# A hybrid decoder step on one core: a second stretch with turned banks, wide tiles counted singly, and an eviction one scan later

## The chip, the core and the metric

One core of a Trainium2 chip runs the whole kernel. The metric is the time of one execution on the device, in microseconds (us). The names of the engines are those of the profile: PE is TensorE (matmuls), PEld its weight loads, DVE is VectorE, ACT ScalarE, POOL GpSimd, SP the engine that issues most transfers.

## What is computed

One layer of a decoder whose mixing width is split in two: windowed attention with query and key norm for one half, a complex diagonal state-space model for the other; then an output projection and a squared-ReLU MLP. All of it in float32, for 256 prompt positions and 8 x 4 sample positions (288 columns in all). Cut to what the change touches:

```python
def hybrid_layer(x, cache_k, cache_v, h0_re, h0_im, p):
    z = rmsnorm(x, p['attn_norm_g']) @ p['w_in']
    q, k, v, u = split_projection(z)
    q = rmsnorm(q, p['q_norm_g'])
    k = rmsnorm(k, p['k_norm_g'])
    ...
    y_ssm, h_re, h_im = ssm_mixer(u, h0_re, h0_im, A_bar, B_bar, ...)
    g = jax.nn.gelu(y_ssm)
    ...

def ssm_mixer(u, h0_re, h0_im, A_bar, B_bar, C_re, C_im, D_skip):
    bu = jnp.einsum('ntgh,gph->ntgp', uf.astype(jnp.complex64), B_bar)
    bu = bu.at[:, 0].add(A_bar * h0)
    _, h = lax.associative_scan(ssm_combine, (a, bu), axis=1)
    y = jnp.real(jnp.einsum('ntgp,ghp->ntgh', h, C)) + D_skip * uf
    ...
```

## The kernel before

**Order of the work.** The kernel is written engine by engine, each with its own instruction list in fixed order, and semaphores between them. Weights arrive in steps of 512 KB in four slots. Up to about 200 us TensorE multiplies in full float32: `gemm_full` (four wide tiles per row of weights) and `gemm_half` (two wide tiles per row of weights, so that a unit's first two PSUM banks fill first, then the other two). A wide tile is one product of a 128 x 128 block of weights with 288 columns; the profile counts it as two matmuls `psum<-x_g,w_raw`. From about 204 us the products run with weights and inputs split into a high and a low part, until the end. The change touches the part between 37 and 164 us.

**PSUM.** PSUM has eight banks. A unit of work (`UNITS`, `UNIT[name]`) takes banks 0 to 3 if its number is even, 4 to 7 if odd. `unit_free` makes TensorE wait, before a unit begins, until the unit two numbers before it has been read (evicted). The units here are, in order: g_u0 (1), bu0 (2), g_u1 (3), g_kv (4), y0 (5), g_q0 (6), bu1 (7), g_q1 (8), kv_aux (9). So g_q1 takes the banks of g_q0.

**The two stretches.** The inputs of the state model, u, are multiplied by B in 32 pairs of state groups, 16 in each stretch: `project_pair(half, n)` makes two small products, real and imaginary, with 32 rows each (`psum<-u_t,b_w` and `psum<-au,b_w`). The profile counts a pair as four matmuls. The first stretch (half 0) goes with the first half of g_u1, the second (half 1) with the first half of g_q0. A pair takes two banks. There are three places for pairs (`PAIR_SLOTS`), which `pair_bank` gives out in turn: two in the unit's own banks, the third borrowed from the second half of the unit beside it, g_u1 or g_q0, which needs these banks only for its own second half. So pair n waits until pair n-3 has been read, and the second half of g_u1 or g_q0 waits for the last pair in the borrowed place (`part_read` ahead of `gemm_half(..., 1, ...)`). Between two such pairs and the next two stand wide tiles:

```python
for m in range(HALF_PAIRS // 2):
    project_pair(1, 2 * m)
    project_pair(1, 2 * m + 1)
    if m < HALF_PAIRS // 2 - 1:
        gemm_half("g_q0", S_Q0, 0, xg3, part=range(2 * m + 2, 2 * m + 4))
part_read(pe, UNIT["bu1"], HALF_PAIRS - 2)
gemm_half("g_q0", S_Q0, 1, xg3)
```

**Who reads the pairs.** VectorE, in `turn_in`: two operations a pair, one into `states`, one into a turn buffer. GpSimd, in `add_turned`, then adds the turn buffer of two pairs to `states` (two operations, `states<-states,turn`), for the first seven of eight such twos; VectorE does the last itself (`add_last`). There are two turn buffers, used in turn, so that VectorE waits, before the pairs 2m and 2m+1, until GpSimd has added those of m-2.

**Behind the second stretch** VectorE scans the states: the sample chunk, then the chunks 0 to 7 (`scan`, per chunk two scans `states<-decay,states`, with a carry of three small operations ahead from chunk 1 on). Among the chunks it evicts g_q0 (`project_out("g_q0", ...)`, the row `q_t<-psum,r_b`) and does the k norm (line 1061). Then `turn_out` makes what TensorE needs for the products with C (`project_states`), whose results `y_out` evicts. TensorE meanwhile does g_q0's second half, the unit kv_aux (means of squares of k, and v transposed) and g_q1.

Of the kernel before, what the change touches and what calls it, by code (L numbers as in the profile page):

```python
# [21 lines left out]
P = 128  # L22
SAMPLE = DEC_BATCH * DEC_SEQ
TOK = SEQ + SAMPLE
KT = D_MODEL // P
# [4 lines left out]
LAST_CHUNK = SEQ // CHUNK - 1  # L30
HALF_PAIRS = PAIRS // 2
# [6 lines left out]
SLOTS = 4  # L38
PAIR_SLOTS = 3
HALF_K, HALF_N = 2 * STEP_K, STEP_N // 2  # L40
# [3 lines left out]
S_U0, S_U1, S_KV, S_Q0, S_Q1, S_GLU = 0, 8, 16, 24, 32, 40  # L44
# [18 lines left out]
UNIT = {name: i for i, (name, _) in enumerate(UNITS)}  # L63
# [68 lines left out]
def build_program(nc, ins, outs):  # L132
    ctx = ExitStack()
    with ctx:
# [78 lines left out]
        raw_half = w_raw[:, :].rearrange("p (s k n) -> p s k n", s=SLOTS, k=HALF_K)  # L213
# [7 lines left out]
        xg3 = x_g[:, :].rearrange("p (k t) -> p k t", t=TOK)  # L221
# [53 lines left out]
        def banks(unit, n=OUTS, cols=TOK):  # L275
            b = 4 * (unit % 2)
            return psum[:, b:b + n, 0:cols]

        def pair_bank(unit, n):
            slot = n % PAIR_SLOTS  # L280
            return 4 * (unit % 2) + 2 * slot if slot < 2 else 4 * ((unit + 1) % 2) + 2


# [96 lines left out]
        def part_read(eng, unit, part):  # L380

            eng.wait_ge(evacuated[unit % 2], evacuations(unit) - UNITS[unit][1] + part + 1)
# [363 lines left out]
        def _(dve):  # L746
# [73 lines left out]
            n = 1  # L820
# [170 lines left out]
            def scan(half, chunks):  # L991
                for c in chunks:
                    if c:
                        carry(half, c)
                    scan_chunk(half, c)
# [54 lines left out]
            for n in range(HALF_PAIRS):  # L1050
# [3 lines left out]
            dve.wait_ge(turn_added, 14)  # L1054
            linked()
            scan_samples(1)
            scan(1, range(3))
            project_out("g_q0", q3[:, 0:4, :])
            scan(1, range(3, 4))
            dve.wait_ge(rsqrt_ready, 1)  # L1060
            nc.vector.scalar_tensor_tensor(kv3[:, 0:2, :], kv3[:, 0:2, :], small[:, SMALL["g_k"]],
                                           sq3[:, 0:2, :], ALU.mult, ALU.mult).then_inc(k_ready, 1)
            scan(1, range(4, LAST_CHUNK + 1))
            turn_out(1, 0)
            q_norm(0, sq3)
            for o in range(1, 4):
# [336 lines left out]
        def _(pe):  # L1403
            def mm(out, lhs_t, rhs, start=True, stop=True):
                return nc.tensor.matmul(out, lhs_t, rhs, start=start, stop=stop)  # L1405
# [40 lines left out]
                    if kk == STEP_K - 1:  # L1446
                        last_mm.then_inc(step_used, 1)

            def gemm_half(name, first_step, half, mov, part=range(KT)):

                if half == 0 and part.start == 0:
                    unit_free(pe, UNIT[name])
                for k in part:
                    n, kk = first_step + half * HALF_STEPS + k // HALF_K, k % HALF_K
                    if kk == 0:
                        pe.wait_ge(raw_loaded[n % SLOTS], (n // SLOTS + 1) * 16)
                    for o in range(2):
                        last_mm = mm(banks(UNIT[name])[:, 2 * half + o, :],
                                     raw_half[:, n % SLOTS, kk, o * P:(o + 1) * P], mov[:, k, :],
                                     start=k == 0, stop=k == KT - 1)  # L1460
                    if kk == HALF_K - 1:
                        last_mm.then_inc(step_used, 1)

            def tiles_ready(signal, before=0, per=1):

# [11 lines left out]
            def project_pair(half, n):  # L1477

                u, j = UNIT[f"bu{half}"], HALF_PAIRS * half + n
                moved = j >= 4  # L1480
                if n % 4 == 0:
                    part_read(pe, UNIT["g_u0"], n // 4) if half == 0 else unit_read(pe, UNIT["g_u1"])
                    if moved:
                        pe.wait_ge(u_moved, j // 4)
                if n == 0:
                    unit_free(pe, u)
                elif n == PAIR_SLOTS - 1:
                    unit_read(pe, u - 1 if half == 0 else UNIT["g_kv"])
                elif n >= PAIR_SLOTS:
                    part_read(pe, u, n - PAIR_SLOTS)  # L1490
                for r in range(2):
                    at = 32 * ((j + 2) % 4) if moved and r else 32 * (j % 4)
                    rows = slice(at, at + 32)
                    src = au3[rows, n // 4, :] if moved and r else u3[rows, j // 4, :]
                    done = mm(psum[:, pair_bank(u, n) + r, 0:TOK], bw4[rows, r, j // 4, :], src)
                done.then_inc(psum_full, 1)
# [93 lines left out]
            for m in range(HALF_PAIRS // 2):  # L1590
                project_pair(0, 2 * m)
                project_pair(0, 2 * m + 1)
                gemm_half("g_u1", S_U1, 0, xg3, part=range(2 * m, 2 * m + 2))
            part_read(pe, UNIT["bu0"], HALF_PAIRS - 2)
            gemm_half("g_u1", S_U1, 1, xg3)
            gemm_full("g_kv", S_KV, GROUP_STEPS, xg3, part=range(12))
# [3 lines left out]
            gemm_full("g_kv", S_KV, GROUP_STEPS, xg3, part=range(14, KT))  # L1600
            project_states(0, 2)
            project_states(0, 3)
            gemm_half("g_q0", S_Q0, 0, xg3, part=range(2))
            for m in range(HALF_PAIRS // 2):
                project_pair(1, 2 * m)
                project_pair(1, 2 * m + 1)
                if m < HALF_PAIRS // 2 - 1:
                    gemm_half("g_q0", S_Q0, 0, xg3, part=range(2 * m + 2, 2 * m + 4))
            part_read(pe, UNIT["bu1"], HALF_PAIRS - 2)
            gemm_half("g_q0", S_Q0, 1, xg3)  # L1610

            pe.wait_ge(const_loaded, 16)
# [302 lines left out]
```

## Time and profile before

| | |
|---|---|
| median of 3 runs | 1175.13 us (1174.14 to 1176.02) |
| the profiled execution | 1174.44 us, its span 1172.6 us |
| PE busy | 1165.6 us, 99% of the span |
| DVE / ACT / POOL busy | 752.3 / 428.0 / 139.2 us |
| chain that ended last | 95% PE, 4% DVE |
| DMA | 190.29 MB, mean 162 GB/s |
| granted TensorE clock | 1.00 |

The span is the time between the first and the last instruction of the profiled execution; the execution's own time is a little longer. The rows are of one execution. The timelines give start and duration of instructions in us from the span's start, with what ended an idle time in brackets. An instruction's duration overlaps with that of the next on its engine, so that the distance between starts is the better measure of pace.

### The profile page before, as it was taken

How to read it: one execution, taken by the hardware profiler on the slowest of the kernel's cores; microseconds unless marked ns; L12 is line 12 of the kernel's file. 1: busy time of each engine (PE TensorE's matmuls, PEld its weight loads, DVE VectorE, ACT ScalarE, POOL GpSimd, SP SyncE). 2: the span in 40 equal slices, each digit the busy share in tenths (PEclk: the TensorE clock that was granted, in tenths of full speed). 3: DMA queues.
4: the chain of work that ended last, by engine and by line, in shares of the span. 5: the costliest groups of instructions: out<-in, count | busy, mean ns of one | idle time of the engine just before them, and what ended most of it. 6: DMA issues, size and time to landing. Idle time of an engine off the chain costs nothing.

```text
span 1172.6 us, 20362 instructions
## 1 busy us (share of the span) xinstructions
PE 1165.6 (99%) x8510; PEld 1101.6 (94%) x8510; DVE 752.3 (64%) x761; ACT 428.0 (36%) x518; POOL 139.2 (12%) x83
## 2 busy tenths in 40 slices
PE   9999999999999999999999999999999999999998
PEld 7676676899999999999999999999999999999998
DVE  7999989989776565554455544555554445555554
ACT  6110033885444334333334333333433332433331
POOL 0512603000000001000001100001100000100000
PEclk9999999999999999999999999999999999999999
DMA  7643334434555544655554455544455555445553
GB/s 292 178 137 108 118 121 158 149 109 147 191 168 178 162 162 144 194 167 162 164 170 152 158 185 171 169 163 162 144 174 186 162 168 171 146 161 182 171 169 117
DMA packets 55192, 190.29 MB, mean 162 GB/s; under 512 B 7864, under 2 KB 10168, under 8 KB 54712
## 3 DMA queue, kind: packets, MB, share of 16 engines
q1 hardware_dynamic: 54824, 188.79, 49.2%
q8 instruction: 67, 1.10, 0.4%
q10 hardware_dynamic: 288, 0.30, 0.1%
q14 instruction: 13, 0.11, 0.0%
HBM read 185.82 MB, written 5.28 MB: 163 GB/s over the span
## 4 chain that ended last, share of the span: by engine, by line
PE 95%; DVE 4%; issue 1%; ACT 0%; POOL 0%; DVEq 0%; POOLq 0%
PE psum L1405 94%; DVE states L967 1%; DVE states L770 0%; DVE out_turn L770 0%; PE psum L1543 0%; DVE out_turn L1009 0%; DVE s_head L1083 0%; DVE q_t L1027 0%; DVE w_lo L761 0%; ACT gate L631 0%; DVE u_t L1021 0%; ACT L553 0%; DVE mov_b L770 0%; DVE q_t L770 0%; DVE stat L1088 0%
## 5 line engine op out<-in xcount | busy, mean ns | idle before, releaser
L761 DVE TENSOR_TENSOR w_lo<-w_raw,w_hi 128x1024 fp32r<-128x1024 f32 x294 | 409.5, 1404 | 385.5 <-ACT w_hi L472 384.7
L1405 PE MATMUL psum<-mov_b,w_hi 128*128 128x288 f32 x2656 | 529.0, 295 | 0.4 <-ACT au L538 0.3
L472 ACT ACTIVATE w_hi<-w_raw 128x1024 fp32r<-128x1024 f32 x294 | 308.3, 1057 | 492.4 <-PE psum L1405 480.6
L1405 PEld LDWEIGHTS psum<-mov_b,w_hi 128*128 128x128 f32 x2656 | 424.8, 188 | 2.5 <-issue 1.0
L1405 PE MATMUL psum<-mov_a,w_hi 128*128 128x288 f32 x2048 | 406.6, 295 | 0.0
L1405 PE MATMUL psum<-mov_b,w_lo 128*128 128x288 f32 x1328 | 390.1, 294 | 0.0
L1405 PEld LDWEIGHTS psum<-mov_a,w_hi 128*128 128x128 f32 x2048 | 327.7, 188 | 0.1
L1405 PE MATMUL psum<-mov_a,w_lo 128*128 128x288 f32 x1024 | 300.7, 294 | 0.0
L1405 PEld LDWEIGHTS psum<-mov_b,w_lo 128*128 128x128 f32 x1328 | 250.6, 189 | 0.0
L1405 PEld LDWEIGHTS psum<-mov_a,w_lo 128*128 128x128 f32 x1024 | 193.3, 189 | 0.0
L1405 PE MATMUL psum<-x_g,w_raw 128*128 128x288 f32 x640 | 162.5, 411 | 1.6 <-DVE turn L770 1.6
L1405 PEld LDWEIGHTS psum<-x_g,w_raw 128*128 128x128 f32 x640 | 120.2, 191 | 42.0 <-issue 8.5
L1345 POOL TENSOR_TENSOR mov_b<-s_relu,mov_b 128x1152 fp32r<-128x1152 f32 x16 | 42.9, 2678 | 536.8 <-ACT mov_b L723 536.8
L1345 POOL TENSOR_TENSOR h_t<-h_t,t_b 128x1152 f32<-128x1152 f32 x15 | 40.1, 2672 | 330.3 <-DVE t_b L770 330.3
L1345 POOL TENSOR_TENSOR states<-states,turn 128x576 f32<-128x576 f32 x28 | 38.8, 1408 | 49.0 <-DVE turn L770 48.3
L723 ACT ACTIVATE mov_b<-s_relu 128x1152 fp32r<-128x1152 f32 x16 | 18.7, 1169 | 63.2 <-DVE s_relu L770 63.2
L967 DVE TENSOR_TENSOR_SCAN states<-decay,states 128x512 f32<-128x512 f32 x32 | 37.4, 1210 | 0.5
L770 DVE TENSOR_TENSOR t_b<-psum,r_b 128x1152 f32<-128x1152 f32 (+1 forms) x19 | 22.1, 1162 | 7.5 <-PE psum L1405 7.5
L1345 POOL TENSOR_TENSOR last<-states,out_turn 128x8 f32<-128x8 f32 (+1 forms) x16 | 15.6, 999 | 92.9 <-DVE states L770 92.9
L770 DVE TENSOR_TENSOR states<-psum,tables 128x576 f32<-128x576 f32 x32 | 24.1, 752 | 2.3 <-PE psum L1405 1.2
L770 DVE TENSOR_TENSOR turn<-psum,tables 128x576 f32<-128x576 f32 x32 | 23.9, 746 | 0.0
L770 DVE TENSOR_TENSOR s_relu<-s_relu 128x1152 f32<-128x1152 f32 x16 | 21.7, 1358 | 0.5
(182 smaller groups left out, 489.0 us busy)
## 6 DMA issues: line engine op xcount, KB each, us to landing
w_raw<-in_w SPq DMA_DIRECT2D x335, 512.0 KB, 3.4
h_t<-in_x SPq DMA_DIRECT2D x3, 576.0 KB, 9.2
out_y<-h_t SPq DMA_DIRECT2D x3, 576.0 KB
b_w<-in_b SPq DMA_DIRECT2D x1, 1024.0 KB, 7.6
c_w<-in_c SPq DMA_DIRECT2D x1, 1024.0 KB, 7.5
k_cache<-in_kc SPq DMA_DIRECT2D x1, 1024.0 KB, 5.9
v_cache<-in_vc SPq DMA_DIRECT2D x1, 1024.0 KB, 6.3
out_kc<-in_kc SPq DMA_DIRECT2D x1, 992.0 KB
```

Of the source, the lines that this page charges most:

```text
L472: nc.scalar.activation(hi3[:, n % SLOTS, :], raw3[:, n % SLOTS, :], ACT.Copy) \
L723: nc.scalar.activation(b4[:, 4 * g:4 * g + 4, 0, :], sr4[:, g % 2, :, :], ACT.Copy) \
L761: nc.vector.tensor_tensor(lo3[:, n % SLOTS, :], raw3[:, n % SLOTS, :], hi3[:, n % SLOTS, :].bitcast(F32), ALU.subtract) \
L770: return nc.vector.tensor_tensor(out, x, y, op)
L967: link(nc.vector.tensor_tensor_scan(st4[:, c, r, :], rate[:, cols], st4[:, c, r, :], 0.0, ALU.mult, ALU.add))
L1345: return nc.gpsimd.tensor_tensor(out, x, y, op)
L1405: return nc.tensor.matmul(out, lhs_t, rhs, start=start, stop=stop)
```

## The change

On TensorE and in the shared helpers:

```diff
@@ -277,7 +277,7 @@
         def pair_bank(unit, n):
-            slot = n % PAIR_SLOTS
+            slot = (n + unit // UNIT["bu1"]) % PAIR_SLOTS
             return 4 * (unit % 2) + 2 * slot if slot < 2 else 4 * ((unit + 1) % 2) + 2
@@ -1446,20 +1446,25 @@
-            def gemm_half(name, first_step, half, mov, part=range(KT)):
-
-                if half == 0 and part.start == 0:
+            def gemm_half(name, first_step, half, mov, tiles=range(2 * KT)):
+
+                if half == 0 and tiles.start == 0:
                     unit_free(pe, UNIT[name])
-                for k in part:
+                for i in tiles:
+                    k, o = i // 2, i % 2
...
+            def quad_tiles(m, ahead=0):
+
+                first = ahead + 7 * m // 2
+                return range(first, ahead + 7 * (m + 1) // 2 if m < HALF_PAIRS // 2 - 1 else 2 * KT)
@@ -1484,7 +1489,7 @@
-                elif n == PAIR_SLOTS - 1:
+                elif n == PAIR_SLOTS - 1 - half:
                     unit_read(pe, u - 1 if half == 0 else UNIT["g_kv"])
@@ -1590,7 +1595,7 @@
                 project_pair(0, 2 * m + 1)
-                gemm_half("g_u1", S_U1, 0, xg3, part=range(2 * m, 2 * m + 2))
+                gemm_half("g_u1", S_U1, 0, xg3, quad_tiles(m))
             part_read(pe, UNIT["bu0"], HALF_PAIRS - 2)
@@ -1600,13 +1605,12 @@
-            gemm_half("g_q0", S_Q0, 0, xg3, part=range(2))
+            gemm_half("g_q0", S_Q0, 0, xg3, range(2))
             for m in range(HALF_PAIRS // 2):
                 project_pair(1, 2 * m)
                 project_pair(1, 2 * m + 1)
-                if m < HALF_PAIRS // 2 - 1:
-                    gemm_half("g_q0", S_Q0, 0, xg3, part=range(2 * m + 2, 2 * m + 4))
-            part_read(pe, UNIT["bu1"], HALF_PAIRS - 2)
+                gemm_half("g_q0", S_Q0, 0, xg3, quad_tiles(m, 2))
+            part_read(pe, UNIT["bu1"], HALF_PAIRS - 3)
             gemm_half("g_q0", S_Q0, 1, xg3)
```

On VectorE, behind the second stretch:

```diff
             scan_samples(1)
-            scan(1, range(3))
+            scan(1, range(4))
             project_out("g_q0", q3[:, 0:4, :])
-            scan(1, range(3, 4))
+            scan(1, range(4, 5))
             dve.wait_ge(rsqrt_ready, 1)
             nc.vector.scalar_tensor_tensor(kv3[:, 0:2, :], kv3[:, 0:2, :], small[:, SMALL["g_k"]],
                                            sq3[:, 0:2, :], ALU.mult, ALU.mult).then_inc(k_ready, 1)
-            scan(1, range(4, LAST_CHUNK + 1))
+            scan(1, range(5, LAST_CHUNK + 1))
```

`gemm_half` now takes single tiles. In the first stretch 3, 4, 3, 4, 3, 4 and 3 wide tiles follow the twos of pairs, and 8 the last, where there were four each time. In the second, 2 tiles stand ahead of the first pairs (before: 4), then 3, 4, 3, 4, 3, 4, 3 and 6 follow (before: 4 seven times, then none). The number of all instructions is as before. In the second stretch pair 0 takes the second place of its own banks, pair 1 the borrowed one, pair 2 the first, and so on; the last pair in the borrowed place is 13 instead of 14.

The list of TensorE where the second stretch begins, before. `x_g,w_raw` are wide tiles, `u_t,b_w` and `au,b_w` a pair:

```order
L1405 MATMUL psum<-x_g,w_raw 128x288 [waits raw_loaded0,evacuated_even]
L1405 MATMUL psum<-x_g,w_raw 128x288 x3
L1405 MATMUL psum<-u_t,b_w 128x288 [waits evacuated_odd,u_moved]
L1405 MATMUL psum<-au,b_w 128x288
L1405 MATMUL psum<-u_t,b_w 128x288
L1405 MATMUL psum<-au,b_w 128x288
L1405 MATMUL psum<-x_g,w_raw 128x288 x4
L1405 MATMUL psum<-u_t,b_w 128x288 [waits evacuated_even]
```

The same place now:

```order
L1405 MATMUL psum<-x_g,w_raw 128x288 [waits raw_loaded0,evacuated_even]
L1405 MATMUL psum<-x_g,w_raw 128x288
L1405 MATMUL psum<-u_t,b_w 128x288 [waits evacuated_odd,u_moved]
L1405 MATMUL psum<-au,b_w 128x288
L1405 MATMUL psum<-u_t,b_w 128x288 [waits evacuated_even]
L1405 MATMUL psum<-au,b_w 128x288
L1405 MATMUL psum<-x_g,w_raw 128x288 x3
L1405 MATMUL psum<-u_t,b_w 128x288
```

Two wide tiles have gone from the front and one from between the pairs, and the wait for the borrowed banks has moved from pair 2 to pair 1.

VectorE's list behind the second stretch, from chunk 2's scans on, as the difference of the two. `q_t` is the eviction of g_q0, `kv_t` the k norm:

```order
 L967 SCALAR_TENSOR_TENSOR states<-decay,states 128x512
+L770 TENSOR_TENSOR carry_p<-carry_e,states 128x64 [waits dve_done]
+L770 TENSOR_TENSOR states<-states,carry_p 128x32 [waits dve_done] x2
+L967 SCALAR_TENSOR_TENSOR states<-decay,states 128x512 [waits dve_done]
+L967 SCALAR_TENSOR_TENSOR states<-decay,states 128x512
 L770 TENSOR_TENSOR q_t<-psum,r_b 128x1152 [waits step_used]
 L770 TENSOR_TENSOR carry_p<-carry_e,states 128x64 [waits dve_done]
```

One chunk's carry and scans have moved ahead of the eviction, and so has one ahead of the k norm, which stands one chunk later too. The lists of ScalarE, GpSimd and SyncE are unchanged.

## Rows read from the trace of the kernel before

**Rows 1.** The page's first part: busy time, share of the span, instructions.

```profile
PE 1165.6 (99%) x8510; PEld 1101.6 (94%) x8510; DVE 752.3 (64%) x761; ACT 428.0 (36%) x518; POOL 139.2 (12%) x83
```

**Rows 2.** All waits of PE: for whom, us in total, times, longest us.

```profile
PE psum L1405 <- DVE turn L770: 1.6, 1, 1.6
PE psum L1405 <- POOL mov_b L1348: 1.3, 1, 1.3
PE psum L1405 <- DVE s_head L1083: 0.5, 1, 0.5
PE psum L1405 <- ACT au L538: 0.3, 1, 0.3
```

**Rows 3.** Timeline of PE, second stretch: start us, us, engine, line, operation.

```profile
118.52 0.51 PE L1405 MATMUL psum<-u_t,b_w 32*128 32x288 f32 x1
...
119.21 2.21 PE L1405 MATMUL psum<-x_g,w_raw 128*128 128x288 f32 x8
121.35 0.51 PE L1405 MATMUL psum<-u_t,b_w 32*128 32x288 f32 x1
...
138.36 0.51 PE L1405 MATMUL psum<-u_t,b_w 32*128 32x288 f32 x1
...
140.71 15.79 PE L1405 MATMUL psum<-x_g,w_raw 128*128 128x288 f32 x64 [1.58 <-DVE turn L770]
156.34 1.13 PE L1405 MATMUL psum<-sq,const 128*128 128x288 f32 x4
...
157.96 11.89 PE L1405 MATMUL psum<-x_g,w_raw 128*128 128x288 f32 x48
```

**Rows 4.** Timeline of PE, end of the first stretch.

```profile
58.42 0.51 PE L1405 MATMUL psum<-u_t,b_w 32*128 32x288 f32 x1
...
59.11 16.27 PE L1405 MATMUL psum<-x_g,w_raw 128*128 128x288 f32 x66
```

**Rows 5.** Timeline of DVE: round 1 of the first stretch, then of the second stretch.

```profile
42.20 0.76 DVE L770 TENSOR_TENSOR states<-psum,tables 128x576 f32<-128x576 f32 x1 [0.49 <-PE psum L1405]
...
119.39 0.76 DVE L770 TENSOR_TENSOR states<-psum,tables 128x576 f32<-128x576 f32 x1 [0.43 <-PE psum L1405]
...
122.15 0.76 DVE L770 TENSOR_TENSOR states<-psum,tables 128x576 f32<-128x576 f32 x1
...
125.06 0.76 DVE L770 TENSOR_TENSOR states<-psum,tables 128x576 f32<-128x576 f32 x1 [0.15 <-PE psum L1405]
...
139.23 0.76 DVE L770 TENSOR_TENSOR states<-psum,tables 128x576 f32<-128x576 f32 x1
```

**Rows 6.** Timeline of POOL, single adds of both stretches.

```profile
45.02 1.41 POOL L1345 TENSOR_TENSOR states<-states,turn 128x576 f32<-128x576 f32 x1 [0.47 <-DVE turn L770]
...
122.22 1.41 POOL L1345 TENSOR_TENSOR states<-states,turn 128x576 f32<-128x576 f32 x1 [7.81 <-DVE turn L770]
123.58 1.41 POOL L1345 TENSOR_TENSOR states<-states,turn 128x576 f32<-128x576 f32 x1
...
127.89 1.41 POOL L1345 TENSOR_TENSOR states<-states,turn 128x576 f32<-128x576 f32 x1
```

**Rows 7.** Timeline of DVE, the fourth turned output behind the first stretch.

```profile
108.42 1.45 DVE L1009 SCALAR_TENSOR_TENSOR out_turn<-states,tables 128x1152 f32<-128x1152 f32 x1 [0.43 <-PE psum L1405]
```

**Rows 8.** Timeline of DVE behind the second stretch.

```profile
152.83 2.34 DVE L967 TENSOR_TENSOR_SCAN states<-decay,states 128x512 f32<-128x512 f32 x2
156.53 1.36 DVE L770 TENSOR_TENSOR q_t<-psum,r_b 128x1152 f32<-128x1152 f32 x1 [1.37 <-PE psum L1405]
...
161.66 0.82 DVE L1061 SCALAR_TENSOR_TENSOR kv_t<-kv_t,small,sq 128x576 f32<-128x576 f32 x1 [0.72 <-ACT sq L553]
```

**Rows 9.** The chain that ended last, around the last eviction of y1: start, us.

```profile
199.87 0.14 issue
200.00 0.50 DVE u_t L1021
```

**Rows 10.** One stretch: length, busy per engine, then PEclk, DMA share, GB/s.

```profile
139.05:140.71 1.66, 0.08 (x4) 0.00 (x1) 1.57 (x4) 0.00 (x0) 1.60 (x3) 1.00 0.77 210
```

More of the change, by code:

```diff
@@ L1447, in gemm_full @@
                         last_mm.then_inc(step_used, 1)
-            def gemm_half(name, first_step, half, mov, part=range(KT)):
-                if half == 0 and part.start == 0:
+            def gemm_half(name, first_step, half, mov, tiles=range(2 * KT)):
+                if half == 0 and tiles.start == 0:
                     unit_free(pe, UNIT[name])
-                for k in part:
+                for i in tiles:
+                    k, o = i // 2, i % 2
                     n, kk = first_step + half * HALF_STEPS + k // HALF_K, k % HALF_K
-                    if kk == 0:
+                    if kk == 0 and o == 0:
                         pe.wait_ge(raw_loaded[n % SLOTS], (n // SLOTS + 1) * 16)
[L1457 to L1462, printed above, removed]
+                    tile_mm = mm(banks(UNIT[name])[:, 2 * half + o, :],
+                                 raw_half[:, n % SLOTS, kk, o * P:(o + 1) * P], mov[:, k, :],
+                                 start=k == 0, stop=k == KT - 1)
+                    if kk == HALF_K - 1 and o == 1:
+                        tile_mm.then_inc(step_used, 1)
+            def quad_tiles(m, ahead=0):
+                first = ahead + 7 * m // 2
+                return range(first, ahead + 7 * (m + 1) // 2 if m < HALF_PAIRS // 2 - 1 else 2 * KT)
             def tiles_ready(signal, before=0, per=1):
```

## The prediction

> **What bounds the kernel now.** I read the page's first part, then who waited for whom on TensorE, then the timelines of TensorE, VectorE and GpSimd around the two places that the diff touches. TensorE is busy 1165.6 of 1172.6 us [rows 1], and all its waits on other engines come to 3.7 us, of which one of 1.6 us lies in what the change touches, and two of 0.3 and 0.5 us shortly behind it [rows 2]. So the kernel is TensorE's own stream, and a change that leaves its work alone can win at most the 2.4 us of those three waits. It can lose whatever new waiting it puts in.
>
> Times below are of the profiled execution, 1174.44 us beside a span of 1172.6 us; the median of the runs shown is 1175.13 us. A difference found in the span is added to the median. 0.2% is 2.35 us, about what a measurement of this kernel can tell from no change.
>
> I call two state-product pairs and the wide tiles behind them a round. A stretch has eight rounds, 0 to 7.
>
> In the second stretch a round takes TensorE 121.35 - 118.52 = 2.83 us [rows 3]: four wide tiles, and about 0.88 us for the two pairs and the changes between the two kinds. A wide tile costs (156.34 - 140.71) / 32 = 0.488 us [rows 3]. VectorE begins a round 0.87 us after TensorE (118.52 to 119.39) and could do one in 122.15 - 119.39 = 2.76 us or a little less [rows 3, 5]. Behind round 7 TensorE stands still until 140.71, for the reading of pair 14 [rows 2, 3].
>
> The row that matters most is GpSimd's. Its two adds of a round take 123.58 + 1.41 - 122.22 = 2.77 us [rows 6]. VectorE may start round m only when GpSimd has added round m-2 (two turn buffers), and GpSimd may add a round only when VectorE has written it. Going round that loop: from VectorE's start to GpSimd's, 127.89 - 125.06 = 2.83 us; the adds, 2.77 us; back to VectorE, 0.07 us (124.99 to 125.06) [rows 5, 6]. That is 5.67 us for two rounds, 2.83 us each. **So TensorE and this loop now run at the same pace, and a quicker TensorE does not make the loop quicker.**
>
> How far can TensorE run ahead? Pair 2m+1 needs the banks of pair 2m-2, read 1.48 us after VectorE began the round before (139.23 to 140.71 [rows 3, 5]). TensorE now comes 2.83 - 0.87 = 1.96 us after that start. It can be 0.48 us earlier, one wide tile, and no more.
>
> **First stretch.** Nothing stood still here: wide tiles follow right behind the last products at 59.11 [rows 4]. Now three and four tiles take turns, and 24 instead of 28 stand ahead of round 7. The four moved behind it cost 4 x 0.488 = 1.95 us there. What TensorE gets for them is the 0.48 us by which it may run ahead, and what the loop itself gains: the first removed tile lets round 1 come earlier, where VectorE and GpSimd had waited 0.49 and 0.47 us [rows 5, 6]. The later rounds keep that start, but no more. The rest, 1.95 - 0.48 - 0.47 = 1.0 us, is new waiting, in rounds 5 and 7 (and a trace of it in 3). The second pair of a round then runs alone and may be 0.1 us shorter, so **+0.95 us**, between 0.85 and 1.0. The lag is not caught up before the second stretch: VectorE, 0.45 us early, runs into products of y0 that TensorE now brings late (it waited 0.43 us for them already [rows 7]), and from there follows TensorE with its full lag.
>
> **Second stretch.** Two tiles less ahead of round 0 let the pair come before VectorE is free, so VectorE starts at 119.39 - 0.43 = 118.96 instead of 119.39 [rows 5], all 0.95 us later by the lag. The loop keeps that and a few hundredths: VectorE ends the stretch 0.45 us earlier than now, before the lag. TensorE's last pair comes 0.48 + 0.40 us earlier, has 38 tiles behind it instead of 32 (6 x 0.488 = 2.93 us), and the stop of 139.05 to 140.71 is gone (1.66 us with the pipe's run-out): -0.88 + 2.93 - 1.66 = +0.4 us. The turned order does what it says: the last use of the borrowed banks is pair 13, read long before those six tiles end. Its wait is gone, but it comes back in eight pieces. Pair 1's new wait, for the eviction of g_kv, is on work done 3 us before: nothing.
>
> **The eviction one scan later.** This is the dearest term. VectorE ends chunk 2 at 152.83 + 2.34 = 155.17, then waits 1.37 us for TensorE, and evicts q_t from 156.53 to 157.89 [rows 8]. TensorE's next unit, g_q1, uses the same banks, and starts at 157.96, 0.07 us behind that [rows 3]. The eviction is already only just in time. With chunk 3 ahead of it (carry and scans up to 161.66 - 0.72 = 160.94, that is 3.1 us from 157.89 [rows 8]) q_t ends at 155.17 + 3.1 + 1.36 = 159.63 and g_q1 starts at 159.70, 1.74 us later than now. With -0.45 us from the stretch and +0.95 us of lag it is **+2.2 us**, at about 160.2. TensorE by itself would be there at 157.96 + 0.4 + 0.95 = 159.3, so a stop of 0.9 us is to be seen. VectorE saves its 1.37 us and the 0.72 us before the k norm [rows 8], and runs some 1.6 us ahead through the scans. That buys nothing: the turned outputs were in time, and from about 185 us on it waits for TensorE's products of y1.
>
> What hands the 2.2 us on: the last piece of y1's eviction starts at 200.00 when TensorE's product is there [rows 9]; from it VectorE goes without a stop to the soft max for which TensorE waits 0.5 us [rows 2]. Both move together, so that wait absorbs nothing. The 0.3 us wait before it shrinks or goes, without effect. The weight loads follow the freed slots, no DMA wait stands in TensorE's list [rows 2], and the k norm, 1.6 us later, feeds a square whose mean TensorE takes 6 us after it now. These cost nothing. Everything behind 257 us is TensorE alone.
>
> **A rule against the change.** The stop of 1.66 us at 139.05 passed at a granted clock of 1.00, the upper of the two levels (2.4 GHz) [rows 10]; I charge no clock for new stops, the longest 0.9 us. The Trainium skill, TensorE: Matmul & The Clock Gate, section A second HAM failure mode, tells of a kernel in which cycling through PSUM banks left TensorE idle for moments between groups, often enough that the clock went back and forth between the levels. Eight short stops in a row, as now made, are that pattern; it is the last rival.
>
> **The sum**: 1.74 - 0.45 + 0.95 = +2.2 us, 1176.6 for a profiled execution and 1177.3 against the median.
>
> **The rivals.**
> - Dearer holds in the first stretch (slower). Place: rounds 3, 5, 7. A product that was held might start its round anew at the price of a change between pairs and tiles, 0.19 us (2.83 - 1.95 - the 0.69 us from 118.52 to 119.21 [rows 3]). Three of them make +0.6 us, 1177.9; a loop slowed likewise, up to 1178.8. It decides from 0.05 us a hold, as only 0.15 us is missing to 0.2%. For it: no hold inside a stretch exists in this trace. Against: TensorE restarted 0.05 us after its releaser at 140.71. In the second stretch such a price would be hidden by the 0.9 us stop.
> - The loop does not bind (VectorE and GpSimd at 2.7 us a round). Then the first lag is 0.1 us, VectorE leaves the second stretch 1.5 us earlier, and g_q1 starts 1.74 - 1.5 + 0.1 = +0.3 us: 1175.4. For it: loop and TensorE tie so exactly that the loop's return of 0.07 us may be TensorE's doing. Against: the adds alone take 2.77 us.
> - The first lag is absorbed, the rest holds: +1.3 us, 1176.4.
> - The stop at 139 goes and nothing takes its place, with one or both waits behind it: -1.6 to -2.4 us, 1173.5 to 1172.7. Against: g_q1's banks wait for q_t.
> - The clock falls for a part of the stretches: each 5 us at the lower level costs 2.5 us, 1179.8. Against: 1.00 in every stretch read.
>
> **How the numbers follow.** The forecast, +1.9 to +2.6 us, has 0.48: 0.30 within 0.2%, 0.18 over it. Dearer holds 0.17, slower. A loop that does not bind 0.15 and an absorbed lag 0.10, both within. The stop gone for nothing 0.07, of which 0.04 faster. The clock 0.03. Faster 0.04, same 0.58, slower 0.38. The range reaches from the third case (1175.4, with some spread to 1175.0) to the dearest loop, 1178.8; outside lie the two last rivals and tails.
>
> **What would show it.** Right: TensorE waiting for VectorE's turn inside both stretches, about 0.5 us in every second round; first wide tile behind the first stretch's last products at 58.1 instead of 59.1, and 40 tiles behind it; GpSimd's adds 2.8 us a round; a wait of 0.9 us for q_t at 160; no wait of VectorE for TensorE before q_t; y1's last eviction at 202.2. Wrong: rounds of 2.6 to 2.7 us on GpSimd, g_q1 starting before 159, or TensorE's clock under 1.00.

## The result, and the profile after

The changed kernel takes 1176.42 us (median of 22 runs, 1175.91 to 1178.41), the kernel before, run beside it, 1174.81 us (22 runs, 1174.06 to 1176.59). The ratio is 1.0014, 95% interval 1.0008 to 1.0020: **1.6 us slower, which is under 0.2%**. Forecast were +2.2 us and a class of no change within 0.2%.

The page's first part of the changed kernel, against [rows 1]:

```profile
PE 1169.4 (99%) x8510; PEld 1104.1 (94%) x8510; DVE 752.2 (64%) x761; ACT 428.4 (36%) x518; POOL 132.5 (11%) x83
```

All waits of its TensorE (for whom, us in total, times, longest us), against [rows 2]:

```profile
PE psum L1405 <- POOL mov_b L1348: 1.3, 1, 1.3
PE psum L1405 <- DMA w_raw<-in_w: 0.7, 1, 0.7
PE psum L1405 <- DVE q_t L770: 0.6, 1, 0.6
PE psum L1405 <- ACT x_g L482: 0.5, 1, 0.5
PE psum L1405 <- DVE s_head L1083: 0.4, 1, 0.4
PE psum L1405 <- ACT au L538: 0.2, 1, 0.2
```

The 1.6 us for the turn have gone, 0.6 us for `q_t` have come. Two rows are not the change's. The waits for `w_raw` and `x_g` lie at the start of the kernel, where nothing was edited (timeline of TensorE, changed kernel: start, us, ...):

```profile
7.86 2.21 PE L1405 MATMUL psum<-x_g,w_raw 128*128 128x288 f32 x8 [0.65 <-DMA w_raw<-in_w]
10.52 19.64 PE L1405 MATMUL psum<-x_g,w_raw 128*128 128x288 f32 x80 [0.45 <-ACT x_g L482]
...
38.33 1.25 PE L1405 MATMUL psum<-u_t,b_w 32*128 32x288 f32 x8
```

The last row is round 0 of the first stretch. It begins at 37.62 in the profiled execution of before, so this one comes 0.71 us late into the part that was changed. VectorE begins the round 1.34 us behind TensorE here and 1.33 us in before (39.67 and 38.95), so both engines are shifted alike. I take 0.71 us off every time of the changed kernel below; "+" is against before. The other foreign part is behind 256 us: the granted clock is at its lower level (1.2 GHz) for about 3.4 us in this execution, which costs 1.5 us. It is told in the last section. With both, the span is 1176.6 us and the execution 1178.41 us, the longest of the 22.

Timeline of TensorE, changed kernel, round 7 of the first stretch and the tiles behind it, against [rows 4]:

```profile
57.63 0.51 PE L1405 MATMUL psum<-u_t,b_w 32*128 32x288 f32 x1
...
58.10 0.51 PE L1405 MATMUL psum<-u_t,b_w 32*128 32x288 f32 x1
...
58.78 42.95 PE L1405 MATMUL psum<-x_g,w_raw 128*128 128x288 f32 x176
```

Where nothing holds a round, its two pairs start 0.02 us apart; here the second comes 0.47 us behind the first. That is a hold. It stands in rounds 5 and 7. The tiles follow at 58.07 after the shift, forecast 58.1.

The second stretch and what follows, against [rows 3]:

```profile
121.51 0.51 PE L1405 MATMUL psum<-u_t,b_w 32*128 32x288 f32 x1
...
121.96 0.51 PE L1405 MATMUL psum<-u_t,b_w 32*128 32x288 f32 x1
...
139.57 18.70 PE L1405 MATMUL psum<-x_g,w_raw 128*128 128x288 f32 x76
158.10 1.13 PE L1405 MATMUL psum<-sq,const 128*128 128x288 f32 x4
...
160.54 11.91 PE L1405 MATMUL psum<-x_g,w_raw 128*128 128x288 f32 x48 [0.65 <-DVE q_t L770]
```

The same hold, 0.45 to 0.47 us, now in rounds 1, 3, 5 and 7. Behind them 38 wide tiles run without a stop. The end of g_q0 (158.10) is +1.05, and g_q1 (160.54) is **+1.87**.

Timeline of VectorE, changed kernel, rounds 0, 2, 4, 6 and 7, then the eviction and the k norm, against [rows 5, 8]:

```profile
120.49 0.75 DVE L770 TENSOR_TENSOR states<-psum,tables 128x576 f32<-128x576 f32 x1
...
126.12 0.76 DVE L770 TENSOR_TENSOR states<-psum,tables 128x576 f32<-128x576 f32 x1 [0.23 <-POOL states L1345]
...
131.76 0.76 DVE L770 TENSOR_TENSOR states<-psum,tables 128x576 f32<-128x576 f32 x1 [0.16 <-POOL states L1345]
...
137.41 0.76 DVE L770 TENSOR_TENSOR states<-psum,tables 128x576 f32<-128x576 f32 x1 [0.17 <-POOL states L1345]
...
140.13 0.76 DVE L770 TENSOR_TENSOR states<-psum,tables 128x576 f32<-128x576 f32 x1
...
159.15 1.33 DVE L770 TENSOR_TENSOR q_t<-psum,r_b 128x1152 f32<-128x1152 f32 x1
...
163.45 0.80 DVE L1061 SCALAR_TENSOR_TENSOR kv_t<-kv_t,small,sq 128x576 f32<-128x576 f32 x1
```

VectorE now waits for GpSimd by name. From 126.12 to 131.76 is 5.64 us for two rounds, 2.82 each: the loop's pace, as forecast. GpSimd keeps the same pace in the first stretch, 19.73 us for its seven rounds (timeline of GpSimd, changed kernel):

```profile
42.50 19.73 POOL L1345 TENSOR_TENSOR states<-states,turn 128x576 f32<-128x576 f32 x14 [40.69 <-DVE turn L770]
```

The waits of VectorE before `q_t` and the k norm are gone. And timeline of VectorE at the end of y1, against [rows 9]:

```profile
202.42 0.52 DVE L1021 SCALAR_TENSOR_TENSOR u_t<-u_t,small,psum 128x288 f32<-128x288 f32 x1 [1.42 <-PE psum L1405]
```

That is 201.71 after the shift, +1.71, and it goes through to the end.

### The profile page after: what moved, and what is told of

It reads as the page before. It is cut to its first block, busy times and chain, and to the rows that moved or that the text cites. A ratio compares the mean times of both kernels' runs of the same rounds, so it can differ in the third digit from the quotient of the medians.

```text
span 1176.6 us, 20362 instructions
## 1 busy us (share of the span) xinstructions
PE 1169.4 (99%) x8510; PEld 1104.1 (94%) x8510; DVE 752.2 (64%) x761; ACT 428.4 (36%) x518; POOL 132.5 (11%) x83
## 4 chain that ended last, share of the span: by engine, by line
PE 94%; DVE 4%; POOL 1%; DMA 1%; issue 0%; ACT 0%; SPq 0%; DVEq 0%
PE psum L1405 93%; DVE states L967 1%; DVE states L770 1%; POOL states L1345 1%; DMA h_t<-in_x 1%; DVE turn L770 1%; PE psum L1548 1%; DVE s_head L1083 0%; DVE w_lo L761 0%; ACT gate L631 0%; DVE q_t L1027 0%; DVE mov_b L770 0%; DVE q_t L770 0%; DVE stat L1088 0%; DVE h_prod L770 0%
## 5 line engine op out<-in xcount | busy, mean ns | idle before, releaser
L1299 DVE TENSOR_SCALAR s_relu<-psum 128x1152 f32<-128x1152 f32 x16 | 21.6, 1351 | 0.0
```

Source lines behind the costliest of these rows:

```text
L1299: nc.vector.tensor_scalar(sr4[:, g % 2, :, :], banks(unit), 0.0, None, ALU.max) \
```

## The experiments

Two quantities are set side by side: the start of g_q1 counted from round 0 of the first stretch in the same execution (120.34 us in before, 157.96 - 37.62), and the time by the ratio to before, whose median is 1174.6 to 1174.8 us in these comparisons. The start of g_q1 is read in one execution of each kernel. VectorE begins round 0 1.33 to 1.34 us behind TensorE in all of them but three: first_only (1.69), second_only (1.86) and after_third (1.48).

The medians mix runs in which TensorE's clock fell for a while with runs in which it did not (last section). The last column takes only runs whose mean granted clock is given as 1.000, and says how far their median lies from that of such runs of before: 1174.39 us, and 1174.50 beside after_early. The 22 runs of before beside the changed kernel have no clock on record; 1174.39 is taken there too.

| kernel | g_q1 | ratio (95%) | median us | at clock 1.000: median, runs, difference |
|---|---|---|---|---|
| changed | +1.87 | 1.0014 (1.0008 to 1.0020) | 1176.42 | 1176.15, 14 of 22, +1.8 |
| turn_only | -1.48 | 0.9988 (0.9979 to 0.9997) | 1173.32 | 1173.21, 7 of 11, -1.2 |
| late_only | +1.67 | 1.0016 (1.0007 to 1.0025) | 1177.07 | 1176.22, 5 of 11, +1.8 |
| turn_late | +1.70 | 1.0026 (1.0016 to 1.0035) | 1177.86 | none of 10 |
| first_only | +1.23 | 1.0006 (0.9997 to 1.0015) | 1175.66 | 1175.58, 7 of 11, +1.2 |
| second_only | +0.21 | 1.0000 (0.9991 to 1.0009) | 1174.93 | 1174.88, 8 of 11, +0.5 |
| after_early | +1.04 | 1.0009 (1.0000 to 1.0018) | 1175.67 | 1175.54, 9 of 11, +1.0 |
| after_third | +0.67 | 1.0001 (0.9992 to 1.0010) | 1174.92 | 1174.92, 9 of 11, +0.5 |
| turn_three | -1.65 | 0.9991 (0.9982 to 1.0000) | 1174.33 | 1172.71, 4 of 11, -1.7 |
| turn_three_lo | -1.65 | 0.9985 (0.9976 to 0.9994) | 1172.76 | 1172.67, 7 of 11, -1.7 |

Where the clock held, the time agrees with the start of g_q1 within 0.3 us in every kernel that has such runs. The mean clock is given to three digits, so a fall of a few tenths of a us in length would not show in it.

**The turned order alone** (turn_only: before, with this).

```diff
-            slot = n % PAIR_SLOTS
+            slot = (n + unit // UNIT["bu1"]) % PAIR_SLOTS
...
-                elif n == PAIR_SLOTS - 1:
+                elif n == PAIR_SLOTS - 1 - half:
...
-            part_read(pe, UNIT["bu1"], HALF_PAIRS - 2)
+            part_read(pe, UNIT["bu1"], HALF_PAIRS - 3)
```

> The kernel before with the turned bank order alone: the last pair in the borrowed banks is 13, the wide tiles stand four by four and the q eviction stays behind chunk 2. My theory (the loop of VectorE and GpSimd sets the pace of the pairs, TensorE may only move work behind them; the order of the banks decides how long it stops behind the last pair): TensorE's stop behind the last products falls from 1.6 to under 0.3 us, g_q0 ends 1.4 us earlier, q_t is evicted at 155.2 without a wait, g_q1 starts 1.3 us earlier, and the time is 1.2 to 1.4 us below before. Rival (stops behind this one are next in line): the gain is taken back at the q eviction or at the soft max, where TensorE waited 0.3 and 0.5 us, and the time falls by less than 0.5 us.

Measured -1.4 us. Its TensorE (timeline, behind round 7) and its VectorE:

```profile
139.37 15.79 PE L1405 MATMUL psum<-x_g,w_raw 128*128 128x288 f32 x64
```

```profile
155.25 1.33 DVE L770 TENSOR_TENSOR q_t<-psum,r_b 128x1152 f32<-128x1152 f32 x1
```

The stop of 1.58 us is gone but for 0.15 us (the tiles start 0.84 us behind the last pairs, which start at 138.53; without a wait it is 0.69), and g_q1 starts at 156.64, 0.06 us behind the end of `q_t` (156.58). So this part wins nearly the whole stop as long as VectorE's eviction keeps its place. It has nothing to spare: a later eviction would hold g_q1 at once.

**The late eviction alone** (late_only: before, with this).

```diff
-            scan(1, range(3))
+            scan(1, range(4))
             project_out("g_q0", q3[:, 0:4, :])
-            scan(1, range(3, 4))
+            scan(1, range(4, 5))
...
-            scan(1, range(4, LAST_CHUNK + 1))
+            scan(1, range(5, LAST_CHUNK + 1))
```

> The kernel before with the q eviction and the k norm one chunk later alone. My theory (g_q1 takes the banks of g_q0, so every us by which VectorE is late there is TensorE's): q_t ends at 159.6, TensorE stops 1.7 us for it and starts g_q1 1.7 us later than before; the time is 1.5 to 1.7 us above before. Rival (the eviction is beside the path, the change's loss is in the stretches): the time is within 0.3 us of before.

Measured +1.9 us by the ratio, a little over the 1.5 to 1.7 expected; its median is 2.45 us above, since six of its eleven runs have a mean clock under 1.000; the other five are 1.8 us above. Timeline of its TensorE, the end of the second stretch and g_q1:

```profile
141.24 15.79 PE L1405 MATMUL psum<-x_g,w_raw 128*128 128x288 f32 x64 [1.58 <-DVE turn L770]
...
160.16 11.91 PE L1405 MATMUL psum<-x_g,w_raw 128*128 128x288 f32 x48 [1.51 <-DVE q_t L770]
```

The old stop stays and a new one of 1.5 us comes: the dearest term, by itself, is +1.67 us at g_q1.

**Both** (turn_late: the two diffs above together).

> The turned bank order as in the run with it alone, and the q eviction and the k norm one chunk later, wide tiles four by four. My theory (the banks of g_q0 decide when g_q1 starts, and VectorE's scans decide when they come free): TensorE ends g_q0 1.4 us earlier and then stops about 3 us for q_t instead of 1.5; g_q1 starts where it does with the late eviction alone, and the whole gain of the turned order is gone: the time is 1.6 to 2.4 us above before, within 0.3 us of the late eviction alone. Rival (the two effects are in different places and add up): 0.3 to 0.6 us above before.

g_q1 starts at +1.70, as in late_only: once the eviction is late, the turned order buys nothing, since VectorE and not TensorE sets when g_q1 may begin. TensorE only waits longer, 3.04 us. The time is +3.0 us, more than expected, and the rows show why. TensorE from there on, and the same stretch with its clock (busy per engine, then PEclk 0.79):

```profile
159.86 14.92 PE L1405 MATMUL psum<-x_g,w_raw 128*128 128x288 f32 x48 [3.04 <-DVE q_t L770]
```

```profile
159.86:174.78 14.92, 14.92 (x49) 11.34 (x50) 14.41 (x23) 2.91 (x3) 0.00 (x0) 0.79 0.21 71
```

The same 48 matmuls took 11.89 us in before [rows 3]. The clock fell still inside the stop and was at its lower level until 166 us (0.50 in each window of one us from 160 to 166, 1.00 from there), for 3.0 us more. This was the profiled execution, at 1179.15 us and a mean clock of 0.997 one of the longest three of ten, which all show 0.997. The other seven lie between 1177.11 and 1178.11 us at 0.999, so they lost less, and none of the ten kept 1.000. The expectation's mechanism holds, as g_q1 shows; its time leaves this out and is too low.

**Single tiles in the first stretch alone** (first_only: before, with the new `gemm_half`).

```diff
-                gemm_half("g_u1", S_U1, 0, xg3, part=range(2 * m, 2 * m + 2))
+                gemm_half("g_u1", S_U1, 0, xg3, quad_tiles(m))
```

> The kernel before with the wide tiles of the first stretch counted singly (3, 4, 3, 4, 3, 4, 3, then 8) alone. My theory: TensorE is held by the loop in rounds 5 and 7 for about 0.45 us each, the first wide tile behind the last products comes 1.0 us earlier but has four more behind it, everything behind is 0.9 us late, and the time is 0.7 to 0.95 us above before. Rival (the lag is absorbed before the second stretch, or the loop does not hold TensorE): under 0.3 us above before.

g_q1 +1.23, of which 0.36 us are this execution's: VectorE began round 0 at 39.31 here and at 38.95 in before, with TensorE at 37.62 in both. The rest is 0.9 us. Time +0.7 us, though the interval reaches down to no change; in the runs at clock 1.000 it is +1.2 us. The lag is already +1.23 us at the last products with C ahead of the second stretch, so it is handed on whole. How large it is in the usual run, 0.9 or 1.2 us, this kernel alone does not show.

**The second stretch alone** (second_only: even tiles in the first stretch, eviction early).

```diff
-            gemm_half("g_q0", S_Q0, 0, xg3, part=range(2))
+            gemm_half("g_q0", S_Q0, 0, xg3, range(2))
...
-                if m < HALF_PAIRS // 2 - 1:
-                    gemm_half("g_q0", S_Q0, 0, xg3, part=range(2 * m + 2, 2 * m + 4))
+                gemm_half("g_q0", S_Q0, 0, xg3, quad_tiles(m, 2))
```

together with the turned order.

> The kernel before with the second stretch as changed (turned banks, 2 tiles ahead, then 3, 4, 3, 4, 3, 4, 3 and 6), the q eviction as before. My theory: TensorE is held inside the rounds and the stop of 1.6 us behind them is gone; g_q0 ends 0.1 to 0.4 us later than before, VectorE waits for it as before, and the time is 0 to 0.4 us above before. Rival (the turned order frees TensorE whatever the tiles): 1 us or more below before, as with the turned order alone.

Time unchanged, g_q1 +0.21. Timeline of its VectorE at the eviction:

```profile
156.29 1.36 DVE L770 TENSOR_TENSOR q_t<-psum,r_b 128x1152 f32<-128x1152 f32 x1 [2.22 <-PE psum L1405]
```

VectorE is earlier than in before and TensorE is not: it waits 2.22 us for TensorE instead of 1.37 [rows 8]. The single stop of 1.6 us has come back as holds and as six more tiles behind the last pair, and the 1.5 us of turn_only are given away.

**The changed kernel with the eviction early** (after_early: the changed kernel, late_only's diff undone).

> The changed kernel with g_q0's eviction and the k norm back in their old places (behind chunk 2 and chunk 3); first and second stretch stay as changed. If the late eviction is the dearest part (theory), VectorE comes to the eviction 1.6 us or more before TensorE's last product of g_q0 and waits for it, TensorE has no stop for q_t, and g_q1 starts with TensorE's own lag alone: 0.9 us of the first stretch and 0.1 to 0.2 us of the second later than in the kernel before, against 1.87 us in the changed kernel. In time some 0.7 to 0.9 us under the changed kernel and 0.8 to 1.2 us above the kernel before. Rival (the eviction costs nothing once the lag is there, since TensorE is late by itself): g_q1 as late as in the changed kernel, 1.87 us, and the same time as the changed kernel. Rival (the lag of the first stretch is mostly absorbed when VectorE is early): g_q1 at most 0.4 us later than before, and the time that of the kernel before.

g_q1 +1.04, time +1.1 us. Its VectorE at the eviction:

```profile
158.28 1.36 DVE L770 TENSOR_TENSOR q_t<-psum,r_b 128x1152 f32<-128x1152 f32 x1 [2.24 <-PE psum L1405]
```

So in the changed kernel TensorE by itself is 1.04 us late, and the eviction adds 0.83 to that. The costs do not add up as 1.67 + 1.04, because g_q1 starts at the later of two sides (VectorE's side holds the lag too, table below). In time the two kernels differ by 0.6 us by the ratios, but their intervals overlap; the rows decide here.

**A third turn buffer** (after_third: the changed kernel, with this).

```diff
+        turn_2, _ = sb("turn_2", 2 * 2 * TOK, at=at_a2)
...
-                if jj == 0 and m >= 2:
-                    dve.wait_ge(turn_added, 7 * half + m - 1)
+                if jj == 0 and m >= 3:
+                    dve.wait_ge(turn_added, 7 * half + m - 2)
...
-                crossed = turn4[m % 2][:, :, ::-1, CHUNK * jj:CHUNK * jj + CHUNK]
+                crossed = turn4[m % 3][:, :, ::-1, CHUNK * jj:CHUNK * jj + CHUNK]
```

GpSimd reads the same three buffers.

> The changed kernel with a third turn buffer, so that VectorE waits for the add of three rounds ago and not of two; nothing else changed. My theory (the loop through two buffers sets 2.82 us a round; without it GpSimd's own 2.75 us does): rounds come every 2.75 us, the holds shrink by some 0.07 us a round, VectorE ends each stretch 0.4 to 0.5 us earlier, and the time is 0.5 to 0.9 us below the changed kernel. Rival 1 (VectorE's own pace or TensorE's is the limit): no change, within 0.2 us of the changed kernel. Rival 2 (the buffers alone held it, GpSimd could go faster): more than 1.2 us below.

This tests whether the loop through two buffers makes the holds. Timelines of its VectorE, two rounds of the first stretch, and of its GpSimd:

```profile
46.89 0.75 DVE L771 TENSOR_TENSOR states<-psum,tables 128x576 f32<-128x576 f32 x1
...
49.55 0.75 DVE L771 TENSOR_TENSOR states<-psum,tables 128x576 f32<-128x576 f32 x1
```

```profile
41.48 19.27 POOL L1346 TENSOR_TENSOR states<-states,turn 128x576 f32<-128x576 f32 x14 [39.66 <-DVE turn L771]
```

VectorE now does a round in 2.66 us, one operation on the heels of the other, instead of 2.82. GpSimd takes 19.27 / 7 = 2.75 us a round instead of 2.82; the third buffer lets it trail. The holds of TensorE in rounds 5 and 7 of the first stretch shrink to 0.07 and 0.14 us. Ahead of the second stretch the lag is 0.29 instead of 0.90 us, and g_q1 is 1.20 us earlier than in the changed kernel. Its median is 1.5 us lower, more than the 0.5 to 0.9 us expected: I had counted on GpSimd's pace, but with a third buffer VectorE's own sets the round. By its number this is the expectation's second rival (more than 1.2 us), but not by its mechanism: GpSimd goes no faster than 2.75 us. The stop for `q_t` is still there, 1.05 us, because TensorE gained more than VectorE.

**The turned order with three tiles ahead** (turn_three: turn_only, and the second stretch as follows).

```diff
+            gemm_half("g_q0", S_Q0, 0, xg3, range(3))
...
+                gemm_half("g_q0", S_Q0, 0, xg3, range(4 * m + 3, min(4 * m + 7, 2 * KT)))
```

> The turned order with 3 wide tiles ahead of the first pair, then four by four and 1 behind the last, evictions as in the kernel before. My theory (TensorE can be one tile ahead of the loop for nothing, and VectorE starts when it is free): VectorE begins the second stretch 0.4 us earlier, no hold comes inside it, the 0.3 us left of the stop behind it goes, g_q1 starts 0.2 to 0.3 us earlier than with the turned order alone, and the time is 1.4 to 1.7 us below before. Rival (what is won here was only exchanged for the q eviction): as the turned order alone, 1.3 us below.

g_q1 -1.65, 0.17 better than turn_only. The median does not show it: four of eleven runs are at 1172.49 to 1172.96 us, all with a mean clock of 1.000, and seven at 1173.93 to 1174.98, all with 0.999. The four lie below every run of turn_only (1173.00 at the least), and their median is 0.5 us under that of turn_only's seven at 1.000, so it seems to beat turn_only where the clock holds. That rests on four runs, and the two kernels ran in different comparisons (before at 1174.39 us in both).

**And two more moves on VectorE** (turn_three_lo): the k norm one chunk later but the eviction in its old place, and the first low part of a weight made before y1's eviction.

```diff
-            scan(1, range(3, 4))
+            scan(1, range(3, 5))
             dve.wait_ge(rsqrt_ready, 1)
...
+            lo_part(EARLY[0])
             y_out(1)
...
-            lo_part(EARLY[0])
             u_los(0)
```

> As the version with 3 tiles ahead, and on VectorE the k norm behind chunk 4 (q eviction stays behind chunk 2) and the first low part of the early weights ahead of y1's eviction instead of behind it. My theory: the 0.7 us wait before the k norm goes, the low part is done in time in which VectorE would wait, and the soft max starts 0.5 to 0.9 us earlier, so that TensorE's 0.4 us stop for it goes: the time is 1.8 to 2.1 us below before. Rival (the low part delays the eviction of q1's squares or y1, and TensorE waits there): no better than 1.5 us below.

The lowest median here: 1172.76 us, 1.8 us under before by the ratio, and by the two ratios 3.4 us under the changed kernel. But the two moves win little of it. The runs at clock 1.000 are as fast as those of turn_three (1172.67 and 1172.71 us); the medians differ because the clock fell in four runs instead of seven. In the waits of its TensorE the one for `s_head` is gone, and one of 0.4 us for `pt_head` has come, which turn_three does not have:

```profile
PE psum L1405 <- POOL mov_b L1348: 1.3, 1, 1.3
PE psum L1405 <- ACT x_g L482: 0.4, 1, 0.4
PE psum L1405 <- ACT pt_head L614: 0.4, 1, 0.4
PE psum L1405 <- ACT au L538: 0.2, 1, 0.2
```

Behind both waits, at 228 us, TensorE is 0.3 us ahead of turn_three in the profiled executions.

## Why the prediction was right, and by how much off

Class, sign and mechanism held, and the time was in the range: 1176.42 us beside a forecast of 1177.3. By the ratio the change costs 1.6 us, forecast 2.2, and that is under the +1.9 to +2.6 us that the forecast's own case was given. The range was wide enough for three rivals as well, and the time is that of one of them, the absorbed lag (1176.4). So the time alone decides nothing; the rows do. Term by term, at g_q1:

| term | forecast | measured |
|---|---|---|
| eviction one scan later | +1.74 | +1.68 (late_only: +1.67) |
| VectorE leaves the second stretch earlier | -0.45 | -0.71 |
| lag of the first stretch | +0.95 | +0.90 |
| start of g_q1 | +2.2 | +1.87 |
| on to y1's last eviction | 0 | -0.16 |

The -0.71 is VectorE at round 7: 140.13 - 0.71 - 139.23 [rows 5] = +0.19, less the lag of 0.90. The +1.68 is what g_q1 adds to that +0.19.

- **The lag.** Right in place and size. Two rounds hold; the trace of a hold forecast for round 3 is not there.
- **The mis-sized term is the -0.45**, "VectorE ends the stretch 0.45 us earlier than now", with "a few hundredths" from the loop. At its start VectorE was 0.51 us earlier (120.49 - 0.71 - 119.39 = +0.39, less 0.90), not 0.43. The rest came inside. With holds the rounds are no longer even: from 126.12, round pairs take 5.64 and 5.65 us, in a long and a short part, and the last round is a short one (137.41 to 140.13, 2.72 us), where before it took 2.83 as the others [rows 5]. That is 0.11 us; the six rounds ahead of it gave 0.09 (16.92 instead of 17.01 us). I had multiplied an even pace. The 0.08 us at the start is the overlap of two operations: 0.43 us was VectorE's idle time [rows 5], and without a wait an operation starts a little before the end of the one ahead (120.49, where the one ahead lasts from 120.15 for 0.43 us).
- **The second stretch of TensorE** cost +0.14 us (1.05 - 0.90; forecast +0.4), for the same reason: its last pair came 1.1 us earlier than before, less the lag, where 0.88 was forecast (138.88 - 0.71 - 0.90 against 138.38). Alone it showed +0.21 (second_only). It did not count, since VectorE's side set the start of g_q1. The stop for `q_t` was 0.65 us by its row; counted by starts, as the forecast's 0.9, it is 1.87 - 1.05 = 0.82.
- **The chain to the end.** "Both move together" missed 0.16 us. The forecast took the start at 200.00 [rows 9] for that of TensorE's product. In before, the four pieces of y1's eviction follow each other at VectorE's own distance, about 0.42 us (the row below, timeline of VectorE, kernel before), which brings the last to 200.00; in the changed kernel it waits 1.42 us for TensorE. So TensorE's product, 1.87 us later, moved the eviction only 1.71. The stop for `s_head` shrank by no more than 0.1 us and took nothing in, as said. With that the two profiled spans are accounted for: 0.71 + 1.71 + 1.5 (the clock behind 256 us) = 3.9 us, measured 1176.6 - 1172.6 = 4.0.

```profile
198.73 1.77 DVE L1021 SCALAR_TENSOR_TENSOR u_t<-u_t,small,psum 128x288 f32<-128x288 f32 x4
```

- **The rivals.** Dearer holds: no. Pairs with a hold take 121.51 to 122.64 = 1.13 us instead of 0.70, that is the hold and nothing more, and the loop kept 2.82 us. A loop that does not bind: no, VectorE names GpSimd before rounds 2, 4 and 6, and a third buffer frees 1.20 us. An absorbed lag: no, although the time is its 1176.4; first_only and after_early hand it on whole. The stop gone for nothing: that is turn_only, which is what the change would have been without its other two parts. The clock: no fall in the stretches, in these rows (columns as in [rows 10]; PEclk 1.00).

```profile
38.00:60.00 22.00, 22.00 (x119) 13.40 (x118) 20.90 (x35) 2.93 (x6) 17.10 (x13) 1.00 0.51 133
...
119.00:140.00 21.00, 21.00 (x115) 12.56 (x115) 20.37 (x33) 0.00 (x0) 16.41 (x12) 1.00 0.33 118
```

The pattern that the Trainium skill describes (TensorE: Matmul & The Clock Gate, A second HAM failure mode: psum-queue depth-cycling) did not set in here: six holds of under 0.5 us in two stretches left the clock at 1.00.

Where did the expected gain go? The turned order wins 1.5 us at g_q1. The single tiles hand it back as holds (second_only: +0.21), the first stretch adds 0.9 us of lag, and the late eviction puts VectorE's side behind TensorE's. Each is seen alone; all meet at one point, the start of g_q1.

## What to carry to other kernels

A unit that takes over banks starts at the later of two sides: the engine that computes, and the one that frees the banks. Work out both before a stop is removed or an eviction is moved. Here a gain of 1.5 us on one side was worth nothing once the other was 1.7 us late, and two harms of 1.67 and 1.04 us made 1.87 together. And where two engines hand a double buffer round, look at the loop's time: work taken out of a third engine's round beyond that turns into holds, which a third buffer took away for the greater part here (lag 0.29 instead of 0.90 us).

## What was not expected of the hardware

**A clock that fell after a long stop.** Stops of 1.5 and 1.6 us left the granted clock as it was in the profiled execution of late_only, which has both. In the one of 3.04 us in turn_late it fell to the lower level, and the 48 matmuls behind took 14.92 us instead of 11.89. One execution shows the place. The ten runs of turn_late lie between 1177.11 and 1179.24 us, none with a mean clock of 1.000, against 1175.59 to 1177.94 for late_only, which starts g_q1 at the same time and kept 1.000 in five of eleven. Whether late_only's other six fell there or behind 256 us is not on record.

**A clock that falls by itself in some executions.** Windows of the changed kernel, with PEclk third from the end:

```profile
256.00:257.00 1.00, 1.00 (x18) 0.97 (x15) 0.69 (x4) 0.86 (x1) 0.00 (x0) 0.90 0.57 139
257.00:258.00 1.00, 1.00 (x7) 1.00 (x6) 1.00 (x1) 0.00 (x0) 0.00 (x0) 0.50 0.95 377
258.00:259.00 1.00, 1.00 (x6) 0.99 (x6) 0.94 (x2) 0.00 (x0) 0.00 (x0) 0.50 0.03 8
259.00:260.00 1.00, 1.00 (x6) 1.00 (x5) 0.99 (x2) 0.00 (x0) 0.00 (x0) 0.50 0.00 0
260.00:261.00 1.00, 1.00 (x10) 1.00 (x9) 1.00 (x3) 0.00 (x0) 0.00 (x0) 0.89 0.00 0
```

TensorE is busy throughout, with no stop. What it did just before are the narrow products of the sample attention (timeline, changed kernel):

```profile
253.86 1.11 PE L1405 MATMUL psum<-pt_samp,v_cache 128*64 128x16 f32 x32
254.90 0.43 PE L1405 MATMUL psum<-pt_new,v_tok 32*64 32x128 f32 x4
255.27 1.11 PE L1405 MATMUL psum<-pt_samp,v_cache 128*64 128x16 f32 x32
256.31 0.53 PE L1405 MATMUL psum<-mov_b,w_hi 128*128 128x288 f32 x2
...
260.81 0.51 PE L1405 MATMUL psum<-mov_b,w_hi 128*128 128x288 f32 x2
```

From the first to the last of these wide rows is 4.50 us. The same two in before, at a clock of 1.00 and behind the same narrow products, are 2.96 us apart:

```profile
253.88 0.54 PE L1405 MATMUL psum<-mov_b,w_hi 128*128 128x288 f32 x2
...
256.84 0.50 PE L1405 MATMUL psum<-mov_b,w_hi 128*128 128x288 f32 x2
```

The dip costs 1.5 us. It stands in the profiled executions of the changed kernel, turn_only, first_only and turn_three, and not in those of before, second_only, late_only, turn_late, turn_three_lo, after_early and after_third. The four that have it show a mean granted clock of 0.999, the others but turn_late 1.000.

The same mean is on record for every run of these kernels. The changed kernel's runs fall in two groups, 0.9 us apart at the least: all six from 1177.6 us are at 0.999, fourteen of the sixteen up to 1176.71 at 1.000. Turn_three's do likewise, without an exception. Before has both as well: 22 of 33 and 23 of 32 runs at 1.000, median 1174.39 us, the rest at 0.999, median 1175.9. So a fall of the clock makes the groups; that it is this dip in each run is likely by its size and not shown, since the mean names no place. It is not of the change's making, since before has it too, and what brings it on was not tried. The narrow products alone do not, as they stand in every execution.

So medians of eleven runs also differ by how many of the runs had the dip, up to 1.5 us a run. To compare versions that are a few tenths of a us apart, runs with the same mean clock have to be set side by side.
